# Reordering three in-order instruction queues in a transformer layer's mixer: bias sums first, group power earlier, a turn one step later

## What is computed

```python
h = rmsnorm(x, norm_mix_pre)
qa, ka, va, qr, kr, vr, gr = split(h @ w_in)          # 7 x 512 columns, 8 heads of 64
ya = softmax(qa ka^T / 8 + t5_bias, causal) @ va      # block-sparse form; dense here (2 blocks)
yr = retention(rotary(qr), rotary(kr) / 8, vr)        # scores * decay, causal
yr = silu(gr) * groupnorm(yr)                         # per head: minus mean, times (var + eps) ** -0.5
x  = x + rmsnorm(concat(ya, yr) @ w_out, norm_mix_post)
u  = conv3(rmsnorm(x, norm_ffn_pre) @ w_up)           # causal, depthwise
x  = x + rmsnorm((gelu(u_gate) * u_val) @ w_down, norm_ffn_post)
```

## Time and profile before

| | us |
|---|---|
| median of 3 runs (lowest, highest) | 647.31 (646.19, 648.04) |
| the profiled execution | 647.02 |
| its span, first to last instruction | 645.2 |
| TensorE busy | 614.3 (95%) |
| VectorE busy | 470.2 (73%) |
| ScalarE busy | 359.2 (56%) |
| GpSimd busy | 142.5 (22%) |
| mean granted TensorE clock | 0.982 |

### The profile page before, as it was taken

The page is one execution under the profiler, slowest core; times in us unless marked ns, Lnnn a source line. Parts: engine busy times, 40 slices in busy tenths (PEclk is TensorE's granted clock), DMA queues, the critical chain, the costliest instruction groups (busy, mean ns, idle before and its releaser), DMA issues.

```text
span 645.2 us, 9451 instructions
## 1 busy us (share of the span) xinstructions
PE 614.3 (95%) x3630; PEld 532.0 (82%) x3630; DVE 470.2 (73%) x678; ACT 359.2 (56%) x563; POOL 142.5 (22%) x147
## 2 busy tenths in 40 slices
PE   8999999979988979799999999999999999899996
PEld 7887887756766756688999999999999998688885
DVE  3521386566665695478895578888889998999886
ACT  5432475355553572367484456766667665666661
POOL 4100221131130210232102222222222223431303
PEclk9999999989988999899999999999999999999998
DMA  8451523223230205738149699889998989997933
GB/s 308 159 158 38 165 63 101 67 64 96 69 97 34 99 22 174 280 130 245 31 99 217 110 200 181 182 152 201 199 183 180 186 168 174 153 199 208 194 135 130
DMA packets 81935, 94.40 MB, mean 146 GB/s; under 512 B 3081, under 2 KB 64185, under 8 KB 81890
## 3 DMA queue, kind: packets, MB, share of 16 engines
q0 software_dynamic: 26352, 35.15, 32.3%
q1 hardware_dynamic: 55538, 58.64, 27.7%
HBM read 91.66 MB, written 2.12 MB: 145 GB/s over the span
## 4 chain that ended last, share of the span: by engine, by line
PE 74%; DVE 13%; ACT 5%; issue 3%; DMA 2%; POOL 1%; DVEq 0%; SPq 0%; POOLq 0%; ACTq 0%
PE bank L708 67%; PE bank L784 1%; PE bank L841 1%; DVE ws L1981 1%; ACT xs L1260 1%; DMA gains<-in_norm_mix_pre_dram 1%; PE bank L719 1%; PE bank L829 1%; DVE ws L1563 1%; DVE xs L1686 1%; DVE yT L1616 1%; DMA raw<-in_w_out_dram 1%; POOL grstd L637 1%; ACT work L1211 1%; DVE xs L1695 1%
## 5 line engine op out<-in xcount | busy, mean ns | idle before, releaser
L708 PE MATMUL bank<-hT,ws 128*128 128x256 f32 (+1 forms) x1416 | 249.6, 332 | 0.2 <-DVE hT L1581 0.2
L708 PEld LDWEIGHTS bank<-hT,ws 128*128 128x128 f32 x1416 | 210.8, 192 | 23.0 <-issue 1.1
L708 PE MATMUL bank<-yT,ws 128*128 128x256 f32 x864 | 106.8, 283 | 0.0
L708 PEld LDWEIGHTS bank<-yT,ws 128*128 128x128 f32 x864 | 105.2, 192 | 0.2
L708 PE MATMUL bank<-ws,hT 128*128 128x512 f32 x432 | 99.9, 390 | 0.0
L708 PE MATMUL bank<-ws,yT 128*128 128x512 f32 x366 | 91.0, 405 | 3.9 <-DVE yT L1957 3.1
L708 PEld LDWEIGHTS bank<-ws,hT 128*128 128x128 f32 x432 | 80.8, 188 | 16.5
L708 PEld LDWEIGHTS bank<-ws,yT 128*128 128x128 f32 x366 | 70.2, 195 | 19.9 <-issue 3.3
L1563 DVE TENSOR_TENSOR ws<-raw,ws 128x1024 fp32r<-128x1024 f32 x47 | 58.7, 1250 | 34.5 <-ACT ws L1130 33.8
L1402 ACT ACTIVATE ws<-raw 128x1024 fp32r<-128x1024 f32 x46 | 48.8, 1060 | 45.8 <-PE bank L708 45.7
L1130 ACT ACTIVATE ws<-raw 128x1024 fp32r<-128x1024 f32 x48 | 50.6, 1056 | 31.2 <-PE bank L708 23.2
(11 more groups left out here) (170 smaller groups left out, 779.4 us busy)
## 6 DMA issues: line engine op xcount, KB each, us to landing
raw<-in_w_in_dram SPq DMA_DIRECT2D x28, 512.0 KB, 3.8
raw<-in_w_up_dram POOLq DMA_DIRECT2D x27, 512.0 KB, 6.1
raw<-in_w_up_dram SPq DMA_DIRECT2D x23, 512.0 KB, 5.8
raw<-in_w_out_dram SPq DMA_DIRECT2D x16, 512.0 KB, 4.4
late<-in_w_up_dram SPq DMA_DIRECT2D x12, 512.0 KB, 5.6
raw<-in_w_down_dram POOLq DMA_DIRECT2D x12, 512.0 KB, 7.8
late<-in_w_up_dram POOLq DMA_DIRECT2D x9, 512.0 KB, 6.1
raw<-in_w_down_dram SPq DMA_DIRECT2D x9, 512.0 KB, 4.1
```

What stands on the lines that cost most here:

```text
L708: return nc.tensor.matmul(dst, st, mv, start=start, stop=stop, skip_group_check=onto)
```

## The change

Four queues are reordered; the work is the same but for eight filler products.

- TensorE: `warm(8)` before the value products goes. `ret_turn_out(i)` moves from b = 12 to b = 13 (steps 30, 45, 59 become 31, 46, 60). In the tail, `ret_mix(last)` moves from piece 12 to 10 and `ret_rows(last)` from 14 to 12.
- ScalarE: `ret_high(i)` moves from b = 13 to b = 14. In the tail, `ret_squares(last)` goes ahead of `split_hi(OUT0 + 7)`.
- VectorE: the one loop over the pairs becomes three: first all `bias_and_max` and `normalise` of the step; then `ret_decay`, `ret_center`, `ret_variance`, `ret_gate` (b = 14 now), `gate_finish`, `ret_norm`; then the stacks, the rotations, `ret_low` (b = 14 now) and `moba_low`. In the tail, `gate_finish` comes ahead of `ret_gate`, the second `ret_decay` ahead of `split_lo(OUT0 + 3)`, `ret_variance` ahead of `split_lo(OUT0 + 6)`, and `ret_norm` ahead of `split_lo(OUT0 + 7)`.
- GpSimd: for i = 1 and 2, `group_rstd(i - 1)` goes ahead of `rotary_sum(i, 1)`; for i = 3 it stays behind it.

```diff
--- before.py
+++ after.py
@@ -660,8 +660,10 @@
                 pool.dma_start(dtab, window(decay.tensor, 2 * i, 2)).then_inc(dtab_loaded, 16)
                 rotary_sum(i, 0)
                 double_keys(ksR, rq_hi, rq_double, i)
+                if i in (1, 2):
+                    group_rstd(i - 1)
                 rotary_sum(i, 1)
-                if i:
+                if i == PAIRS - 1:
                     group_rstd(i - 1)
             group_rstd(PAIRS - 1)
 
@@ -861,7 +863,6 @@
             turn_rows(0)
             warm(2)
             turn_rows(1)
-            warm(8)
 
             for n in range(2):
                 pe.wait_ge(w_hi, n + 1)
@@ -925,7 +926,7 @@
                             ret_mix(i)
                         if b == 6:
                             ret_rows(i)
-                        if b == 12:
+                        if b == 13:
                             ret_turn_out(i)
                     if a in (0, 2, 4, 6):
                         moba_scores(i, a)
@@ -978,9 +979,9 @@
                     ret_scores(last, e - 1)
                 if e == 4:
                     moba_mix(last)
+                if e == 10:
+                    ret_mix(last)
                 if e == 12:
-                    ret_mix(last)
-                if e == 14:
                     ret_rows(last)
                 if e == 24:
                     ret_turn_out(last)
@@ -1296,15 +1297,15 @@
                         ret_stack(i, 0)
                     if g == END[QR, i] + 1:
                         swap_halves(i, QR)
-                    if b == 13:
+                    if b == 14:
                         ret_high(i)
                     if g == END[QR, i] + 4:
                         ret_stack(i, 1)
                 if g % 3 == 1:
                     split_hi(VALUES + g // 3 + 2)
+            split_hi(OUT0 + 2)
 
             last = PAIRS - 1
-            split_hi(OUT0 + 2)
             gate_halftanh(last)
             copy_turned(last, 6)
             copy_turned(last, 7)
@@ -1315,8 +1316,8 @@
             split_hi(OUT0 + 5)
             ret_copy(last)
             split_hi(OUT0 + 6)
+            ret_squares(last)
             split_hi(OUT0 + 7)
-            ret_squares(last)
             split_hi(OUT0 + 8)
             ret_high(last)
             split_hi(OUT0 + 9)
@@ -1706,52 +1707,56 @@
 
             for g in range(STEPS):
                 for i in range(PAIRS):
+                    a = g - BLOCKS_FROM[i]
+                    if a in (1, 3, 5, 7):
+                        bias_and_max(i, a - 1)
+                        bias_and_max(i, a)
+                    if a in (2, 4, 6, 8):
+                        normalise(i, a - 2)
+                        normalise(i, a - 1)
+                for i in range(PAIRS):
                     a, b = g - BLOCKS_FROM[i], g - RETENTION_FROM[i]
-                    if g == END[GR, i] + 1:
-                        gate_finish(i)
                     if b in (0, 1, 2, 3):
                         ret_decay(i, 2 * b)
                         ret_decay(i, 2 * b + 1)
+                    if b == 7:
+                        ret_center(i)
+                    if b == 10:
+                        ret_variance(i)
+                    if b == 14:
+                        ret_gate(i)
+                    if g == END[GR, i] + 1:
+                        gate_finish(i)
+                    if b == 11:
+                        ret_norm(i)
+                for i in range(PAIRS):
+                    a, b = g - BLOCKS_FROM[i], g - RETENTION_FROM[i]
                     if g == END[KA, i] + 1:
                         moba_stack(i, 0)
                     if g == END[QA, i] + 1:
                         moba_stack(i, 1)
-                    if a in (1, 3, 5, 7):
-                        bias_and_max(i, a - 1)
-                        bias_and_max(i, a)
                     if g == END[KR, i] + 1:
                         rotate(i, KR)
-                    if b == 10:
-                        ret_variance(i)
-                    if b == 13:
-                        ret_gate(i)
-                    if a in (2, 4, 6, 8):
-                        normalise(i, a - 2)
-                        normalise(i, a - 1)
-                    if b == 7:
-                        ret_center(i)
-                    if a == 12:
-                        moba_low(i)
-                    if b == 11:
-                        ret_norm(i)
                     if g == END[KR, i] + 4:
                         ret_stack(i, 0)
                     if g == END[QR, i] + 2:
                         rotate(i, QR)
-                    if b == 13:
-                        ret_low(i)
                     if g == END[QR, i] + 4:
                         ret_stack(i, 1)
+                    if b == 14:
+                        ret_low(i)
+                    if a == 12:
+                        moba_low(i)
                 if g % 3 == 2:
                     split_lo(VALUES + g // 3 + 2)
+            split_lo(OUT0 + 2)
 
             last = PAIRS - 1
-            split_lo(OUT0 + 2)
+            gate_finish(last)
             ret_gate(last - 1)
-            gate_finish(last)
             ret_decay(last, 0)
+            ret_decay(last, 1)
             split_lo(OUT0 + 3)
-            ret_decay(last, 1)
             ret_low(last - 1)
             ret_decay(last, 2)
             ret_decay(last, 3)
@@ -1763,10 +1768,10 @@
             split_lo(OUT0 + 4)
             split_lo(OUT0 + 5)
             ret_center(last)
+            ret_variance(last)
             split_lo(OUT0 + 6)
-            ret_variance(last)
+            ret_norm(last)
             split_lo(OUT0 + 7)
-            ret_norm(last)
             split_lo(OUT0 + 8)
             ret_gate(last)
             ret_low(last)
```

## The result

The changed kernel took 630.89 us in the median of 4 runs (629.54 to 631.90), the kernel before 647.67 us beside it (646.19 to 648.55). The ratio is 0.9742, with a 95% interval of 0.9712 to 0.9772: 2.6% faster, 16.8 us. The forecast was 630.6 us.

What follows compares the result with a forecast made beforehand. TensorE, busy 614.3 of 645.2 us, was taken as the bound, with 18.7 us of waits and 9.6 us of half clock recoverable. Terms 1.7 + 0.4 + 5.3 + 4.0 + 0 + 5.0 = 16.4 us, 647.0 to 630.6 us; range 624.5 to 637.

Steps and rivals of the forecast that it cites:

- The start: Ahead of the value products: without the eight fillers TensorE goes on from 12.25 us; gain 1.7 us.
- Step 16: gate_finish no longer stands before the two probabilities TensorE is about to turn; gain 0.4 us.
- The first turn: Steps 24 to 33: waits of 5.7 us become 2.25 and the clock's fall goes; gain 5.3 us.
- rival (c): GpSimd's power blocks VectorE in two turns, costing 1.4 us: 632.0 us; 8 in 100.
- The second turn: Steps 39 to 47: waits of 5.1 us become 3.05, one of two clock falls stays; gain 4.0 us.
- The third turn and piece 3: Steps 53 to 60 and first output products: waits 4.6 become 5.05 us, with a fall behind 3.1; net 0.
- The tail: After the mixer: the 3.37 us norm wait and half clock go, ret_rows waits 1.15 us; gain 5.0 us.
- Rival (a): Remaining waits are too short for the clock to fall, so both kept falls go: 627.2 us; 15 in 100.
- (b): New stops in the in-order queues are each 1 to 1.5 us longer, with a further fall: 636 us; 25 in 100.
- (d): The mixer's gain is eaten later because weights do not come sooner: 645 to 647 us; 3 in 100.
- (e): Slower: without the fillers TensorE starts its products at half clock: 649 us and more; 3 in 100.

Runs made afterwards that it cites:

- u_warm: The changed kernel with warm(8) put back ahead of the value products; ratio 0.9777 to the kernel before.
- r_same: The changed kernel measured once more with no edit; 634.58 us, ratio 0.9792 to the kernel before.
- u_tail: The changed kernel with all of the tail's order as before; ratio 0.9799 to the kernel before.
- f_split3: The changed kernel with split_hi(OUT0 + 3) directly behind split_hi(OUT0 + 2), and split_lo(OUT0 + 3) ahead of gate_finish and ret_gate; ratio 0.9693 to the kernel before.
- f_high: The changed kernel with ret_high and ret_low one step later still (b = 15); ratio 0.9703 to the kernel before.
- f_early: The changed kernel with copy_turned(i, 4) and (i, 5) moved ahead of the last exponents on ScalarE; ratio 0.9738 to the kernel before.
- u_pool: The changed kernel with GpSimd's old order, rotary_sum(i, 1) ahead of group_rstd(i - 1) in every turn; ratio 0.9797 to the kernel before.
- f_all: The changed kernel with f_split3, f_high, ret_copy(last) ahead of split_hi(OUT0 + 5), and ScalarE's ret_stack(i, 1) ahead of its step's exponents; 623.99 us, ratio 0.9628.
- u_loop: The changed kernel with VectorE's single loop over the pairs back, ret_gate and ret_low at b = 14; ratio 0.9782 to the kernel before.
- f_best: The changed kernel with all parts of f_all and the early copies of f_early; 621.88 us, ratio 0.9615 to the kernel before.

## Why the prediction was right

**The start** was right in mechanism and place: 1.8 us up to ret_mix(0) for 1.7, and u_warm shows the 1.7 alone.

**Step 16** was right in the step and wrong in the sum. Counted from the first value product, the products behind the turn there start 0.3 us sooner (82.1 us behind it, 82.4 before), but a wait of 0.48 us follows at step 18 that was not there before, for the copy of the same pair:

```profile
93.49 0.82 PE L831 MATMUL bank<-ident,xs 128*128 128x128 f32 x6
...
99.35 1.06 PE L831 MATMUL bank<-ident,xs 128*128 128x128 f32 x8 [0.48 <-ACT work L1253]
```

What TensorE won it gave back two steps later, as ScalarE and VectorE came no sooner. Net 0 in place of 0.4.

**The first turn** went as worked out. The power starts right behind the variance, and the norm waits for the rotary sum's end. Timeline of the changed kernel, to be laid beside the earlier trace rows:

```profile
131.00 1.68 POOL L637 TENSOR_TENSOR grstd<-gms,neghalf 128x8 f32<-128x8 f32 x1
...
131.05 0.69 DVE L1706 TENSOR_TENSOR work<-work,rot 128x512 f32<-128x512 f32 x1
...
132.66 1.28 POOL L641 TENSOR_TENSOR work<-work 128x512 f32<-128x512 f32 x1
...
132.71 1.78 DVE L1662 TENSOR_TENSOR work<-work,grstd 128x512 f32<-128x512 f32 x1
...
142.80 0.63 ACT L1235 ACTIVATE yT<-work 128x512 fp32r<-128x512 f32 x1 [0.41 <-DVE work L1667]
...
143.34 0.85 ACT L1253 ACTIVATE work<-bank 128x384 f32<-128x384 f32 x2
...
143.96 1.06 PE L831 MATMUL bank<-ident,xs 128*128 128x128 f32 x8 [2.08 <-ACT work L1253]
```

The norm (L1662) begins 0.05 us after the sum (L641) and takes 1.78 us, where it took 0.69 before: it ends 0.55 us after the sum, as if it had stood still for most of it. rotate's second half (L1706, two SBUF operands) runs in 0.69 us beside the power (L637): rival (c) is out. The Trainium skill (SBUF — State Buffer, Who interferes with whom) has the first case right and would have had the second take until 132.7 at least; the measurement decides. (The slip in the prediction's working changes nothing: the split of 1.39 us beside the power in the earlier trace rows is the query's, not the key's.) The last three rows are the third wait: ret_high ends, the copy follows, TensorE had waited 2.08 us (forecast 1.75). The other waits of the turn were 0.42 and 0.46 us (0.3 and 0.2). In sum 5.0 for 5.3.

**The second turn** has the forecast's two waits, at the forecast's places:

```profile
182.26 1.25 ACT L1202 ACTIVATE qsR<-work 64x512 fp32r<-64x512 f32 x2
...
183.55 1.39 DVE L1619 TENSOR_TENSOR qsR<-work,qsR 64x512 fp32r<-64x512 f32 x2 [2.14 <-ACT qsR L1202]
...
184.99 0.50 PE L774 MATMUL bank<-qsR,ksR 128*128 128x512 f32 x1 [2.25 <-DVE qsR L1619]
...
187.13 1.25 PE L831 MATMUL bank<-ident,xs 128*128 128x128 f32 x8 [0.94 <-DVE xs L1696]
```

2.25 and 0.94 us (1.95 and 1.1 forecast), the query split behind ScalarE's half of it behind the exponents. The term was mis-sized by 1.4 us, 5.4 for 4.0, because the one fall of the clock that I kept did not come in this execution. It came in all six later profiles with this pair of waits (r_same, u_warm, u_tail, f_split3, f_high, f_early) and in u_pool's with 3.17 and 0.90 us, in three of the seven about twice as long; so the term stands for an average execution, and its reason, "a gap of 2.14 us was followed by a fall", was too firm for a single one.

**The third turn and piece 3**: 1.25, 1.09 and 2.97 us for 0.8, 1.15 and 3.1, with the fall behind the last. **The tail**: no wait at ret_turn_out (256.44 at full clock, the 81 products in 18.64 us against the forecast's 18.8), 1.00 us before ret_rows for 1.15:

```profile
222.60 0.66 PE L802 MATMUL bank<-ident,work 128*128 128x128 f32 x4 [1.25 <-DVE work L1662]
...
224.35 1.07 PE L831 MATMUL bank<-ident,xs 128*128 128x128 f32 x8 [1.09 <-ACT work L1253]
...
231.36 0.98 PE L710 MATMUL bank<-ws,yT 128*128 128x512 f32 x3 [2.97 <-DVE ws L1564]
...
247.76 0.66 PE L795 MATMUL bank<-ident,work 128*128 128x128 f32 x4 [1.00 <-ACT work L1225]
```

Together 4.9 for 5.0: up to ret_mix(3), which now stands 1.4 us earlier in the queue, 1.2 us are saved, so that this part lost 0.2 us where 0 was forecast, and the tail gained 5.1 for 5.0. **Rival (a)**, neither fall, came in no profile of the changed kernel: of its two falls one came in the first, one in r_same, and r_same had another late in the down product. **(b)**, longer stops, did not come in the first measurement (the stops that the forecast named came to 12.5 us for its 11.5). Its 636 us are nearer to the four unprofiled runs of r_same at 634.6 than the forecast is, but their mean clock of 0.987 speaks for the clock and not for the queues. **(d)** and **(e)** are out by the window of 259 to 497 us and by u_warm.

That the sum is off by 0.7 us in the span is partly luck: -0.4 and -0.3 at two places, +1.4 at a third. The five falls of the kernel before cost 9.8 us and the one after 1.7, so 8.1 of the 17.1 us are clock. That shorter waits bring fewer falls is clear in the first turn alone: the clock fell in both profiles that have the wait of 3.1 us there, and in none of the twelve with waits of at most 2.1 us. Over a whole execution it does not hold from profile to profile: f_all waited 6.2 us less than the changed kernel and lost 3.1 us more by the clock, and r_same with the same waits lost 3.0 us and not 1.7. So the clock's share of the gain is that of one execution. Which fall comes in a given one cannot be worked out from one trace.

## What to carry to other kernels

In in-order queues a move is priced by what it puts behind and ahead of every instruction it passes, on each engine: a wait taken off TensorE comes back one or two steps later unless its cause, too, comes sooner (step 16, f_early), and a rule of order that pays in two turns need not in a third (u_loop). A wait of one to three us of TensorE can cost more than its length, since the clock may fall behind it (1.4 to 1.7 us each time here); ask for the next wait's releaser until only short waits are left. Where falls come by chance, compare stretches between fixed points of several profiles, with the lost clock set apart, before believing a median.

## What was not expected of the hardware

The same program with the same waits to 0.1 us had the granted clock fall to 0.50 at different places: behind 2.25 and 0.94 us not at all in one execution, for about 3 us in another (r_same, 1.5 us lost), for twice that in programs with the same pair (u_warm, f_early); behind a wait of 2.97 us once and once not; behind waits of 1.24 and 1.09 us in u_warm, u_pool and u_turn and not behind the same two in the changed kernel, r_same, u_tail, f_split3, f_high and f_all; behind a lone wait of 1.54 us in f_all and not behind the 1.56 us of f_best. A lone wait of 2.08 us in the first turn brought none in any of six profiles. Each single fall lost 1.4 to 1.7 us. Two measurements of the one program thus lay at 0.9742 and 0.9792, whose intervals hardly meet. Falls also came late, in the down product (540 to 560 us of r_same at 0.91), in some profiles and not in others.
